# Keeping the residual of a two-layer streaming encoder turned (channels on partitions), with weights stationary in the output and down products

## The reference, cut to what matters

```python
for i in range(DEPTH):                                   # DEPTH = 2
    n = rms_norm(x, ln1_w[i]);  proj = n @ w_in[i]       # 1024 -> 3584: q k v g, B C h
    ret_out = silu(g) * group_norm(retention(rope(q), rope(k), v, state))
    conv_out = B * conv3(C * h)
    x = x + concat([ret_out, conv_out]) @ w_out[i]       # 1024 -> 1024
    h2 = rms_norm(x, ln2_w[i])
    x = x + square(relu(h2 @ w_up[i])) @ w_down[i]       # 1024 -> 4096 -> 1024
y = rms_norm(x, ln_f_w)
# rms_norm(x, w) = x * rsqrt(mean(x*x, -1) + 1e-6) * w
```

## Time and profile before

| what | value |
|---|---|
| median of 3 runs (range) | 1339.78 us (1339.36 to 1339.87) |
| the profiled execution, its span | 1337.8 us |
| PE busy | 1324.8 us (99%) |
| PEld busy | 1201.9 us (90%) |
| DVE busy | 1004.4 us (75%) |
| ACT busy | 684.4 us (51%) |
| POOL busy | 174.8 us (13%) |
| granted clock of PE, 40 slices | 9 in each (in tenths, 9 is 90% or more) |
| chain that ended last | PE 98% |

### The profile page before, as it was taken

The page is one execution under the profiler, slowest core; times in us unless marked ns, Lnnn a source line. Parts: engine busy times, 40 slices in busy tenths (PEclk is TensorE's granted clock), DMA queues, the critical chain, the costliest instruction groups (busy, mean ns, idle before and its releaser), DMA issues.

```text
span 1337.8 us, 19242 instructions
## 1 busy us (share of the span) xinstructions
PE 1324.8 (99%) x7718; PEld 1201.9 (90%) x7718; DVE 1004.4 (75%) x1191; ACT 684.4 (51%) x835; POOL 174.8 (13%) x176
## 2 busy tenths in 40 slices
PE   8999999999999999999999999999999999999997
PEld 6889999899899899899888899988998988988986
DVE  6547888898867867858875477898988588587586
ACT  5314545477446446446532255455764464564464
POOL 2622011020000000000034211011100000000001
PEclk9999999999999999999999999999999999999999
DMA  8473676556445454455144746656654635635523
GB/s 279 123 234 71 167 139 145 159 110 165 140 107 154 129 118 135 126 127 157 32 128 136 210 88 157 159 105 164 137 147 126 149 104 131 153 95 142 142 63 110
DMA packets 113823, 182.67 MB, mean 137 GB/s; under 512 B 4740, under 2 KB 36612, under 8 KB 113736
## 3 DMA queue, kind: packets, MB, share of 16 engines
q1 hardware_dynamic: 82792, 126.59, 28.5%
q0 software_dynamic: 30656, 54.53, 24.4%
q10 hardware_dynamic: 288, 0.33, 0.1%
HBM read 174.02 MB, written 7.41 MB: 136 GB/s over the span
## 4 chain that ended last, share of the span: by engine, by line
PE 98%; DMA 0%; ACT 0%; issue 0%; POOL 0%; DVE 0%; SPq 0%; DVEq 0%; POOLq 0%; ACTq 0%
PE pair L947 44%; PE pair L1039 28%; PE pair L771 12%; PE pair L1052 8%; PE pair L822 2%; PE pair L842 1%; PE pair L846 1%; PE pair L851 1%; DMA w_raw<-in_w_in 0%; PE pair L854 0%; PE pair L864 0%; PE pair L877 0%; POOL rstd L1673 0%; DVE xn L1834 0%; PE pair L858 0%
## 5 line engine op out<-in xcount | busy, mean ns | idle before, releaser
L1275 ACT ACTIVATE ring<-raws 128x1024 fp32r<-128x1024 f32 x304 | 318.5, 1057 | 338.7 <-PE pair L947 149.4
L2026 DVE TENSOR_TENSOR ring<-raws,ring 128x1024 fp32r<-128x1024 f32 x304 | 368.2, 1221 | 138.7 <-ACT ring L1275 138.3
L947 PE MATMUL pair<-mlp_in_hi,ring 128*128 128x320 f32 x1792 | 396.6, 309 | 0.0
L1039 PE MATMUL pair<-ring,a_ring 128*128 128x512 f32 x1680 | 392.3, 390 | 0.0
L1039 PEld LDWEIGHTS pair<-ring,a_ring 128*128 128x128 f32 x1680 | 314.1, 188 | 65.8 <-issue 0.7
L947 PEld LDWEIGHTS pair<-mlp_in_hi,ring 128*128 128x128 f32 x1792 | 300.1, 188 | 0.8
L947 PE MATMUL pair<-mlp_in_lo,ring 128*128 128x320 f32 x896 | 276.7, 309 | 0.0
L947 PEld LDWEIGHTS pair<-mlp_in_lo,ring 128*128 128x128 f32 x896 | 168.2, 188 | 0.2
L947 PE MATMUL pair<-ch_in_hi,ring 128*128 128x320 f32 x512 | 112.9, 308 | 0.0
L1979 DVE TENSOR_TENSOR x<-x,pair 128x512 f32<-128x512 f32 x160 | 103.6, 682 | 11.7 <-PE pair L1039 11.7
L771 PE MATMUL pair<-pair_a,norm_hi 128*128 128x512 f32 x320 | 100.5, 395 | 0.3 <-ACT norm_hi L1183 0.3
(11 more groups left out here) (190 smaller groups left out, 1599.2 us busy)
## 6 DMA issues: line engine op xcount, KB each, us to landing
raws<-in_w_mlp_up SPq DMA_DIRECT2D x32, 1024.0 KB, 5.7
raws<-in_w_mlp_down SPq DMA_DIRECT2D x32, 1024.0 KB, 5.3
raws<-in_w_in SPq DMA_DIRECT2D x16, 1024.0 KB, 6.1
raws<-in_w_mlp_up POOLq DMA_DIRECT2D x16, 1024.0 KB, 9.5
raws<-in_w_mlp_down POOLq DMA_DIRECT2D x16, 1024.0 KB, 8.7
w_raw<-in_w_in SPq DMA_DIRECT2D x11, 1024.0 KB, 8.1
past_state<-in_state_ret SPq DMA_DIRECT2D x16, 512.0 KB, 7.3
raws<-in_w_in POOLq DMA_DIRECT2D x8, 1024.0 KB, 9.4
```

The lines of the kernel that those rows point to most:

```text
L947: mm = pe.matmul(out[:, n, 0:HALF], item_half(item, h, a)[:, k, n * P:(n + 1) * P], tokens[c][:, k], start=(i in (B11, B21, SUM_1112) and ...
L1039: mm = pe.matmul(out[:], a_item[:, a, 2 * h + k, pair * P:(pair + 1) * P], item_half(item, h, c)[:, k], start=(i in (B11, B21, SUM_1112) a ...
L1275: nc.scalar.activation(item_half(item, h, 0), raw_half(quad, RAW_OF[i], h), ACT.Copy).then_inc(half_hi.sem, 1)
L2026: nc.vector.tensor_tensor(item_half(item, h, 1), raw_half(quad, RAW_OF[i], h), f(item_half(item, h, 0)), ALU.subtract).then_inc(half_lo.se ...
```

## The change

- **x stays turned.** It is loaded turned by the host (`x_turned`, `[128, 8, 640]`: channels on partitions, tokens along), lives so, and is stored so (`y_turned`). The transposes of both norms go; those of k, q, o and the small states stay.
- **Down and output products** (`down_half`) have weights stationary and 320 token columns moving, for all 640 tokens in Strassen's scheme: 336 matmuls a stage. `down_sample` and its operands go. There are 14 adds of 640 elements, and activation items are 1280 wide instead of 1024. Products B21, SUM_1112 and B22 go to one pair of banks (`down_other`), the others to another.
- **Order of products** is now B11, B21, 1112, 111222, B22, 1222, ALL.
- **Sums of squares** run over partitions now: ACT squares (128x640 each), POOL adds them up (`add_squares`, 12 adds of 320 in a norm; the last two are DVE's, `add_last_squares`), PE multiplies by a matrix of ones (one fp32 matmul of 320 columns, `sum_rows`), DVE transposes 32x32 blocks of the result and adds the epsilon (`mean_rows`), POOL takes the power of 10 columns (`root_rows`), DVE spreads it over the partitions (`spread_root`). In layer 0 the first norm works in token slices 0:128, 128:320, 320:640, later in halves of 320.
- **First norm:** DVE scales (`scale_rows`), ACT and DVE make the high and low parts for the MIX stage.
- **Second norm:** x is only multiplied by the norm weights (`weigh_rows` on POOL, 3 x 1280 elements; `weigh_21` on DVE) and goes unscaled into the up products. The root is multiplied in at the relu, which moves to DVE (`relu_quarter`, `relu_last`); ACT squares only.
- `turn(("tail",))` moves from `down(OUT)` into the last OUT up product, and the warming matmuls at the start go from 7 to 12, on a matrix of ones. The loads of the rows of norm weights go.

The core of the diff:

```diff
-B11, B21, SUM_1112, SUM_111222, SUM_1222, B22, SUM_ALL = range(PRODUCTS)
+B11, B21, SUM_1112, SUM_111222, B22, SUM_1222, SUM_ALL = range(PRODUCTS)
...
-    out = {B21: bank_b, SUM_1112: bank_c, B22: bank_c}.get(i, bank_a)[pair]
-    a_item = a_ring[:, (a_to(b, i) - 1) % 2]
-    for k in range(2):
-        for m, (a, c) in enumerate(three):
-            mm = pe.matmul(out[:], a_item[:, a, 2 * h + k, pair * P:(pair + 1) * P],
-                           item_half(item, h, c)[:, k], ...)
+    out = (down_other if i in (B21, SUM_1112, B22) else down_chain)[h]
+    a_item = a_ring[:, (a_to(b, i) - 1) % 2]
+    for n in range(2):
+        for k in range(4):
+            for m, (a, c) in enumerate(three):
+                mm = pe.matmul(out[:, n, 0:HALF], item_half(item, h, a)[:, k, n * P:(n + 1) * P],
+                               a_item[:, c, k], ...)
...
+def down_banks(b, i, h):
...
+    read = {SUM_1112: B21, SUM_111222: B11, B22: SUM_1112, SUM_1222: SUM_111222,
+            SUM_ALL: SUM_1222}[i]
+    pe.wait_ge(x_added.sem, x_added.at(layer, x_adds_to(b, read, h)))
...
+def sum_rows(kind, layer, t):
+    pe.wait_ge(acc_step.sem, acc_step.at(squares_at(kind, layer), BEHIND_SQUARES[4 * t + 3]))
+    pe.matmul(sum_bank[t][:, 0:HALF], ones[:], acc[:, t], start=True, stop=True).then_inc(sums_ready, 1)
...
+def root_rows(n, width):
+    pool.wait_ge(mean_ready, n + 1)
+    nc.gpsimd.tensor_tensor(root_of[:, cols], mean_of[:, cols], minus_half[:, cols], ALU.pow
...
+def weigh_rows(layer, n):
+    to, dh, t = ((t11, 0, 0), (t12, 1, 0), (t22, 1, 1))[n]
+    pool.wait_ge(x_added.sem, x_added.at(layer, x_adds_to(OUT, (B21, B22, SUM_1222)[n], 1)))
+    nc.gpsimd.tensor_tensor(to[:], x[:, 4 * dh:4 * dh + 4, t * HALF:(t + 1) * HALF],
+                            weight_cols(layer, 1, 4 * dh, 4, HALF), ALU.mult)...
...
+def relu_quarter(b, i):
+    dve.wait_ge(hidden_summed.sem, hidden_summed.at(layer, c_sums_to(b, i, 1)))
+    dve.wait_ge(root_spread, norm_of("n2", layer, t) + 1)
+    nc.vector.scalar_tensor_tensor(out=hh, in0=hh, scalar=0.0, in1=spread(t, 4), op0=op, op1=ALU.mult
...
-    act.wait_ge(hidden_summed.sem, hidden_summed.at(layer, c_sums_to(b, of, 1)))
-    nc.scalar.activation(hh, hh, ACT.Relu, scale=scale).then_inc(quarter_relu.sem, 1)
     act.wait_ge(quarter_relu.sem, ...)
     nc.scalar.activation(hh, hh, ACT.Square).then_inc(hidden_ready.sem, 1)
```

More of the change, by code:

```diff
@@ L170, in mlp_steps @@
     for b in range(OUT, NBLK):
[L171 to L178, removed]
+        out += [(kind, b, i, h) for kind in ("up", "down") for i in range(PRODUCTS) for h in range(2)]
     return out
@@ L190, in half_used, with x_adds_to @@
         return STEP["up", (quad - 3) // 2 if quad >= 2 else quad - 2, i, h]
[L191 to L203, removed]
+    return STEP["down", quad // 2 - 2, i, h]
+def x_adds_to(b, i, h):
+    return (b + 1) * X_ADDS + 2 * i + h + 1
 def a_to(b, i):
@@ L777, in turn @@
                 kind = what[0]
-                last = n - 2 if kind != "n2" else n - 4 if what[1] in (2, 4) else -1
+                last = n - 2
                 if kind == "tail":
@@ new lines, in square_rows @@
+            def square_rows(kind, layer, n):
+                t, dh, h = SQUARES[n]
+                b, of = (OUT, layer) if kind == "n2" else (NBLK - 1, layer - 1)
+                i = ((B21, B22), (SUM_ALL, SUM_1222))[t][dh]
+                act.wait_ge(x_added.sem, x_added.at(of, x_adds_to(b, i, h)))
+                if n >= 2:
+                    act.wait_ge(acc_step.sem, acc_step.at(squares_at(kind, layer), BEHIND_SQUARES[n - 2]))
+                nc.scalar.activation(squares_of[kind][:, n % 2], x_rows(dh, h, t), ACT.Square, scale=MEAN
+                                     ).then_inc(squares.sem, 1)
@@ L1154, in read_turn, with rows_hi @@
+            def rows_hi(layer, s, pair):
+                first, last = SLICES[layer][s]
+                act.wait_ge(xn_ready, rows_to(layer, s, pair))
+                nc.scalar.activation(norm_hi[:, 2 * pair:2 * pair + 2, first:last], xn[:, pair, :, 0:last - first], ACT.Copy
+                                     ).then_inc(n1_hi, 1)
             def read_turn(layer, what):
@@ L1642, in _ @@
[L1642 to L1650 removed]
+                    rows_hi(layer + 1, 0, 0)
@@ new lines, in _ @@
+                    rows_lo(layer + 1, 1, ROW_PAIRS - 1)
+            mean_rows(norm_of("end", DEPTH, 0), HALF, 0)
+            add_to_x(DEPTH - 1, NBLK - 1, SUM_ALL, 0)
+            spread_root(norm_of("end", DEPTH, 0), 0, HALF)
+            for two in range(ROW_PAIRS):
+                finish_rows(0, two)
+            add_to_x(DEPTH - 1, NBLK - 1, SUM_ALL, 1)
+            add_last_squares("end", DEPTH)
+            mean_rows(norm_of("end", DEPTH, 1), HALF, 1)
+            spread_root(norm_of("end", DEPTH, 1), HALF, TOK)
@@ L2504, in shape_constants @@
+            for two in range(ROW_PAIRS - 1):
+                finish_rows(1, two)
 def shape_constants():
```

1277 lines of the change are left out of this document (588 added, 689 removed).

## The result

| | before | after |
|---|---|---|
| median | 1339.59 us (4 runs) | 1435.81 us (4 runs, 1435.43 to 1437.89) |
| ratio | | 1.0721, 95% interval 1.0706 to 1.0737 |
| span of the profiled execution | 1337.8 us | 1433.6 us |
| PE busy | 1324.8 (99%) | 1354.2 (94%) |
| mean granted clock of PE | 0.998 | 0.968 |

A forecast was written before the change was run, and what follows sets the result against it. The prediction took PE's own work to bound the kernel. Its terms, PE work down 11.3 us and the rest waiting, summed to +51.7 us on 1339.8, giving 1391.5 us, with a range of 1345 to 1412.

The forecast's parts named there:

- Down products: Down stages: 336 matmuls of 320 columns take 49.26 us against 49.20 before, +0.7 us over ten stages.
- Transposes and ones: PE's own work: dropped transposes of the norms save 16.7 us, new fp32 products with the ones matrix cost 4.7.
- The wait for B21's add: Each of ten down stages: PE waits 2.2 us before SUM_1112 until B21's first half is added to x, +22 us.
- a rival with a chance of 0.10: Clock falls after waits: 1.7 us of half-pace matmuls behind each of ten down waits and four seams, +24, 1415 us; chance 0.10.
- The seam: Between output product and first up stage: late B21 inputs, late first hidden sum, POOL against DVE; 9.0 us a layer, +18.
- The head: Start of the kernel: first norm's chain queued on DVE delays V to 51.3 to 51.7 us, +12 us.
- Between the layers: Before layer 1's first K group: sum, root, spread and scale passes outlast SUM_ALL's 7.04 us on PE, +3.7 us.
- The tail: From last matmul to the end: 14.3 us instead of 7.0, +7.3 us.
- The rival on the ports: POOL's passes fall on DVE in full: 2 x (5 to 8) us more, 1402 to 1408 us; chance 0.10.

The follow-up runs named there:

- e_down: Changed kernel with DVE's order in the down stages rewritten, both B21 adds ahead of the next half weight and the difference: 1410.96 us.
- e_later: Changed kernel with B21's first add in each down stage one DVE pass (1.14 us) later: 1450.28 us.
- e_fill: Changed kernel with ten small fp32 products of a matrix of ones put before SUM_1112 in each down stage: 1427.54 us.
- e_fill5: Changed kernel with five small products of ones before SUM_1112 in each down stage, in place of the ten of e_fill: 1427.80 us.
- e_thin: Changed kernel with ten of POOL's twelve adds of squares in the norms behind output product and layer 8 columns wide instead of 320: 1430.93 us.
- e_seam2: Changed kernel with a second reordering of POOL, ACT and DVE between output product and first up stage, ones product moved to B21: 1432.12 us.
- e_act: Changed kernel with reordered down stages, head, tail and seam (e_down, e_seam2 included), second norm's row weighing moved from POOL to ACT: 1384.30 us, ratio 1.0335.
- e_seam: Changed kernel with a first reordering of POOL, ACT and DVE between output product and first up stage: 1450.09 us.

## Why the prediction was wrong, point by point

1. **Down products, +0.7:** right in kind. 49.41 (e_down) against 49.20 is +0.2 a stage, 2 in all.
2. **Transposes and ones, -12.0:** not measured alone, and not contradicted. With waits and slow matmuls taken off, the output product has 49.9 us (52.9 before) and the first up stage 50.0 (51.3 before), 8.4 less in both layers; the up stages of OUT, which got a turn from there, have 1.0 more.
3. **The wait for B21's add, +22:** right, 2.20 us in each of ten stages; e_later moved it by the 1.14 of one pass, e_down took it away. The profile's table called its cause "issue" instead of L1874.
4. **What follows the wait:** this is the step that failed. The sum priced a wait at its own length. Behind eight of the ten down waits, and behind those of head and seams, came matmuls at half the pace: 1.5 us in each of the six stages down 1 to 3 and in both output products, some 28 us in the whole kernel with the head and the seams. That is the largest part of the 44.5 us by which the forecast was short. I had it as a rival with a chance of 0.10, argued away with "waits of 2 us are shorter than 4.45"; its price (1.7) and total (24) were near. In down 0 of both layers the same 2.2 us had no such consequence; e_fill and e_fill5 show that the slow matmuls come from PE standing still, but not what decides whether a given wait brings them.
5. **The seam, +18:** 11.3 us of waits per layer where 9.0 was forecast, and 6 us of slow matmuls. The places were right (inputs of B21, B21's first hidden sum); besides them ACT's squares, which wait for adds (5.5 and 2.0 us), stood before a half weight and the item of SUM_ALL and held it up.
6. **The head, +12:** V starts 16.8 us after the 39.7 that I took as free of waits. DVE ended its rows at 42.9 instead of 39.4, and the first K groups ran at half pace (0.43 us between matmuls of 512 columns): again the clock.
7. **Between the layers, +3.7:** some 6 us of waits and 3 of slow matmuls.
8. **The tail, +7.3:** +13.1 (20.10 against 7.03). Mis-sized because I counted the passes behind the last add and not those ahead of it: eight finished rows, 7.3 us. "What is queued ahead of the late instruction" was the question that step 8 did not ask.

The rival on the ports is right in kind: DVE passes held up by POOL are in the rows. Its size is bounded only: thinner adds, which also shorten POOL's own chain, brought 12 us in the reordered kernel and 5 in the changed one.

Open: why 2.2 us of waiting were followed by the lower clock in down 1 and not in down 0. It is not the stage: with the same wait of 2.20, down 0 of layer 0 has the slow stretch in e_thin (53.09), and down 1 of layer 0 has none in e_seam2 (51.56). What else decides, no run here was made to show. Open too is what of the remaining 45 us of e_act could go. Against before, its head (V at 52.0 for 42.4), its first up stages (58.1 and 57.4 for 51.3) and its end (68.7 from the start of the last down stage for 56.4) hold some 35 of them.

## What to carry to other kernels

When a change lets PE wait where it never waited, price each wait twice: its length, and behind it the matmuls at half pace (here 1.5 us behind eight of ten waits of 2.2 us, and nothing, 1.5 or 2.6 us behind waits of 3.3). With queues in a fixed order, work out for the instruction that is waited for what stands ahead of it on its engine, and then look for the pass that waits itself with something urgent behind it: in e_seam a few passes moved wrongly cost the first up stage 14 us, twice what the new order won in the output product. POOL is not free help for DVE: wide two-operand passes go better to ACT where a layout allows it.

## What the runs showed of the hardware that I had not expected

- Behind ten waits of 2.2 us in the down and output products, 12 or 13 matmuls at 0.267 us in place of 0.147 came in eight stages and none in two (granted clock 0.60 over 4.25 us in down 1). Behind ten waits of 1.0 us at the same places (e_fill5) none came directly; behind ten of 3.3 us (e_later) 10 to 13 came in six stages, 19 to 21 in three and none in one.
- The lower clock can begin some matmuls behind the wait: in down 1 six started at the full clock first (475.07 to 475.88), in down 2 of e_later none.
- Ten matmuls of 128 columns by a matrix of ones, with no use for the result, kept the clock at 1.00 in place of the 2.2 us wait, and so did five with 1.0 us of standing still (down 1, 51.54 us in both).
- POOL's power takes 1.02 us for 4 columns, 1.60 for 6 and 1.98 for 10, and a DVE pass beside POOL's two-operand passes can last almost three times its own time (4.29 for 1.49).
